# Two transformer blocks in one kernel: order of gelu and weight splits, order of the second mixer's end, and two border orders

## What is computed

```python
# first block, per layer
x = x + 0.5 * swiglu(rms(x), w_gu, w_down)         # D_FF = 2816
x = x + hybrid_mixer(rms(x))                       # gMLP branch + top-k attention, gated, @ w_out
x = x + 0.5 * swiglu(rms(x), w_gu2, w_down2)
# second block, per layer
h = mixer_2(rms(x)); x = x + rms(h)
h = conv_glu_ffn(rms(x)); x = x + rms(h)
# mixer_2
q, k, v = l2norm/silu(causal conv of 4 taps)       # gated delta rule, 4 heads of 128
o_a = rmsnorm(delta_rule(q, k, v, g, beta)) * silu(z)
o_b = softmax(q k^T / 8 + reach) v                 # 8 heads of 64, dilated attention folded into one bias
h = concat([o_a, o_b]) @ w_out
# conv_glu_ffn
gate, val = split(causal conv of 3 taps (h @ up) + bias)
h = (gelu(gate) * val) @ down
```

## Time and profile before

| | |
|---|---|
| median of three runs | 2065.92 us (2065.55 to 2076.42) |
| the profiled execution | 2066.17 us |
| its span, first to last instruction | 2064.3 us |
| mean granted TensorE clock | 0.964 of full speed |
| PE busy | 1919.4 us |
| DVE, ACT, POOL busy | 1223.1, 996.8, 652.8 us |
| second block, stage gu, layer 0 | about 1401 to 1532 us of the span |
| second block, from side's last tile to out, layer 0 | 1310.8 to 1353.8 us |
| the same in layer 1 | gu 1855 to 1985, side to out 1764.7 to 1807.7 us |

### The profile page before, as it was taken

The page is one execution under the profiler, slowest core; times in us unless marked ns, Lnnn a source line. Parts: engine busy times, 40 slices in busy tenths (PEclk is TensorE's granted clock), DMA queues, the critical chain, the costliest instruction groups (busy, mean ns, idle before and its releaser), DMA issues.

```text
span 2064.3 us, 41181 instructions
## 1 busy us (share of the span) xinstructions
PE 1919.4 (93%) x15758; PEld 1870.1 (91%) x15758; DVE 1223.1 (59%) x1478; ACT 996.8 (48%) x1304; POOL 652.8 (32%) x595
## 2 busy tenths in 40 slices
PE   6999999999999999999999989879999889779997
PEld 6999999999989999999999989769889789679897
DVE  4655586666456456866664674446664664356655
ACT  5434456544444345564444563445544564445543
POOL 4751301276137513012662016122330025032220
PEclk9999999999999999999999899989999799889999
DMA  6646444465455464444555422114445222124444
GB/s 221 209 164 210 154 144 145 162 206 193 164 195 201 157 215 164 144 146 159 206 190 168 154 102 100 42 64 144 175 144 199 90 102 87 37 82 163 166 164 159
DMA packets 49222, 314.39 MB, mean 152 GB/s; under 512 B 5713, under 2 KB 6865, under 8 KB 19921
## 3 DMA queue, kind: packets, MB, share of 16 engines
q1 hardware_dynamic: 48960, 311.09, 43.7%
q10 hardware_dynamic: 144, 1.69, 0.2%
HBM read 311.71 MB, written 1.05 MB: 152 GB/s over the span
## 4 chain that ended last, share of the span: by engine, by line
PE 62%; DVE 10%; issue 9%; ACT 9%; DMA 5%; POOL 2%; ACTq 1%; DVEq 0%; SPq 0%; POOLq 0%
PE ps L541 15%; PE ps L543 15%; PE ps L542 15%; DMA raw<-in_down_dram 4%; ACT w_hi L1109 4%; DVE w_lo L1567 4%; PE ps L858 3%; PE ps L546 3%; PE ps L547 3%; PE ps L548 3%; DVE conv L1886 2%; ACT conv L1160 2%; PE ps L691 1%; PE ps L731 1%; DVE v L2084 1%
## 5 line engine op out<-in xcount | busy, mean ns | idle before, releaser
L1567 DVE TENSOR_TENSOR w_lo<-raw,w_hi 128x2048 fp32r<-128x2048 f32 (+1 forms) x322 | 713.0, 2215 | 423.6 <-ACT w_hi L1109 423.1
L541 PE MATMUL ps<-xn,w_hi 128*128 128x256 f32 x2688 | 768.5, 286 | 59.6 <-DVE w_lo L1567 14.6
L542 PE MATMUL ps<-xn,w_hi 128*128 128x256 f32 x2688 | 755.7, 281 | 0.0
L543 PE MATMUL ps<-xn,w_lo 128*128 128x256 f32 x2688 | 755.5, 281 | 0.0
L1109 ACT ACTIVATE w_hi<-raw 128x2048 fp32r<-128x2048 f32 (+1 forms) x322 | 562.4, 1748 | 126.5 <-DMA raw<-in_down_dram 83.4
L541 PEld LDWEIGHTS ps<-xn,w_hi 128*128 128x128 f32 x2688 | 516.9, 192 | 74.2 <-issue 44.1
L542 PEld LDWEIGHTS ps<-xn,w_hi 128*128 128x128 f32 x2688 | 515.4, 192 | 0.8 <-issue 0.5
L543 PEld LDWEIGHTS ps<-xn,w_lo 128*128 128x128 f32 x2688 | 515.1, 192 | 0.0
L541 PE MATMUL ps<-h,w_hi 128*128 128x256 f32 x1056 | 294.1, 278 | 4.9 <-DVE w_lo L1567 4.8
L542 PE MATMUL ps<-h,w_hi 128*128 128x256 f32 x1056 | 293.2, 278 | 0.0
L543 PE MATMUL ps<-h,w_lo 128*128 128x256 f32 x1056 | 293.2, 278 | 0.0
(11 more groups left out here) (310 smaller groups left out, 2633.2 us busy)
## 6 DMA issues: line engine op xcount, KB each, us to landing
raw<-in_gu_dram SPq DMA_DIRECT2D x132, 1024.0 KB, 4.9
raw<-in_in_dram SPq DMA_DIRECT2D x70, 1024.0 KB, 4.9
raw<-in_down_dram SPq DMA_DIRECT2D x96, 704.0 KB, 4.1
raw<-in_out_dram SPq DMA_DIRECT2D x16, 1024.0 KB, 4.8
raw<-in_pb_dram SPq DMA_DIRECT2D x4, 1024.0 KB, 4.8
raw<-in_pa_dram SPq DMA_DIRECT2D x4, 1024.0 KB, 4.9
tables_all<-in_tables_dram ACTq DMA_DIRECT2D x1, 1648.0 KB, 7.2
rows<-in_rows_dram SPq DMA_DIRECT2D x2, 768.0 KB, 5.5
```

Of the source, the lines that this page charges most:

```text
L541: pe.matmul(out, w, xh, start=first, stop=False)
L542: pe.matmul(out, w, xl, start=False, stop=False)
L543: return pe.matmul(out, wl, xh, start=False, stop=last)
L1567: dve.tensor_tensor(w_lo[:, r, 0:elems], raw[:, k % RAW_RING, 0:elems], w_hi[:, r, 0:elems], ALU.subtract).then_inc(lo.sem, 1)
```

## The change

It has three parts. **Gelu:** `rounds` runs the body of slot j first and splits slot j+3 behind it, with one split ahead of the loop (`open_rounds`); that is the same sequence as before. What ACT has left of the body, `behind`, comes after the split: in the second block the gelu of slot j now stands behind the split of slot j+3. In the first block `open_rounds` stands ahead of ACT's root of the norm. **Mixer's end:** the units' early steps move into side's last two slots; the short units get the banks 0 to 3 and their own halves of `soft` and `p_t`; z's silu is one instruction behind `attend_exp(1)`, followed by a load of the Exp table; slots 2 and 3 of out are split ahead of the out stage; the sums over heads stand ahead of the last attention transposition, and Ln, Exp, gain and high part go by halves; PE begins out with the attention half of slots 0 to 2 in six banks, then does their delta-rule half, then slot 3 whole. The short units' helpers (`short_scores`, `short_turn`, `short_pv`, `short_mask`, `short_exp`, `short_copy`) do what the old ones did, in the other banks and buffers. **Border orders:** `tile_rounds` splits slot 2j+4 ahead of taking tile j, and takes the last two tiles behind the first split of the next stage; in the first block's out stage the split comes ahead of both tiles and the low part of tile c-1 behind the addition of tile c.

```diff
+        if k == 6:
+            attend_turn(at, 0, SC)
+        if k == 7:
+            attend_scores(at, 1, 4, SC)
...
+    def out_part(j, first, end):
+        for f in range(2):
+            if j == 3:
+                pe.wait_ge(x_new.sem, x_new.upto(at, so.free0 + f + 1))
+            for c in range(first, end):
+                if j == 0 and f == 0 and c == WC:
+                    pe.wait_ge(o_lo.sem, o_lo.upto(at, 1))
+                if j == 0 and f == 0 and c == WC + 2:
+                    pe.wait_ge(o_lo_last.sem, o_lo_last.upto(at, 1))
+                last = mac(out_tile(2 * j + f), wh[:, c, f * P:(f + 1) * P], wl[:, c, f * P:(f + 1) * P],
+                           y2[:, c, 0], y2[:, c, 1], c == 0, c == KC - 1)
+            if end == KC:
+                last.then_inc(used.sem if f else full.sem, 1)
...
+    def head_sums():
+        for b in range(2):
+            pe.matmul(ps[:, AUX + b, :], ones_q[:], q_diag[:, 2 * b:2 * b + 2].rearrange("p h q -> p (h q)"),
+                      start=True, stop=False)
+            pe.matmul(ps[:, AUX + b, :], ones[:],
+                      o_sq[:, 2 * b:2 * b + 2].rearrange("p h q -> p (h q)"), start=False, stop=True)\
+              .then_inc(o_summed.sem, 1)
...
         if k == 7:
-            attend_pv(at, 0, tok[:, V], SC)
             level_u(LEVELS - 1)
-            attend_scores(at, 1, 4, SC)
+            short_scores(at, 2)
+            short_scores(at, 3)
...
     heads4(AUX, lambda i: v_new[:, 0, i], lambda i: qk[:, 0, i], dn_out)
-    attend_out(at, 1, SC)
+    short_turn(at, 2)
     pe.wait_ge(dn_copy.sem, dn_copy.upto(at, 4))
-    attend_scores(at, 2, 4, SC)
...
     last.then_inc(dn_out.sem, 1)
-    attend_turn(at, 2, SC)
-    attend_pv(at, 2, tok[:, V], SC)
-    attend_scores(at, 3, 4, SC)
-    pe.wait_ge(q_diag_ok.sem, q_diag_ok.upto(at, 2))
-    pe.wait_ge(o_squared.sem, o_squared.upto(at, 1))
...
-    attend_turn(at, 3, SC)
-    attend_pv(at, 3, tok[:, V], SC)
-    attend_out(at, 0, SC)
-    stage_open(at, ss)
-    pe.wait_ge(o_lo.sem, o_lo.upto(at, 1))
+    attend_out(at, 1, SC)
+    short_turn(at, 3)
+    short_pv(at, 2, tok[:, V])
+    short_pv(at, 3, tok[:, V])
+    head_sums()
+    attend_out(at, 0, SC + 1)
     pe.wait_ge(yb_lo.sem, yb_lo.upto(at, 2))
-    for j in range(4):
-        wide(at, so, j, 0, y2, KC)
+    out_part(0, 0, WC)
+    out_part(1, 0, WC)
+    out_part(2, 0, WC)
+    for j in range(3):
+        out_part(j, WC, KC)
+    out_part(3, 0, KC)
@@ helpers
+    def open_rounds(at, st, split):
+split(at, st.slot0 + LEAD, 0, st.elems)
+    def rounds(eng, at, st, nxt, count, split, body, behind=None):
 def step(j, g):
-    for s in range(per):
-        split(at, st.slot0 + per * j + LEAD + s, g, st.elems)
     body(j, g)
+    split(at, st.slot0 + j + 1 + LEAD, g, st.elems)
+    if behind:
+        behind(j, g)
+cycle(eng, count - LEAD - 1, RING, step)
+for j in range(count - LEAD - 1, count):
     body(j, 0)
-    if last:
-        split(at, st.slot0 + per * j + LEAD + per - 1, 0, nxt)
+    if j == count - LEAD - 1:
+        split(at, st.slot0 + j + 1 + LEAD, 0, nxt)
+    if behind:
+        behind(j, 0)
+split(at, st.slot0 + count - 1 + LEAD, 0, nxt)
+    def tile_rounds(eng, at, st, nxt, split, body, steps=cycle):
+def step(j, g):
+    split(at, st.slot0 + 2 * j + 1 + LEAD, g, st.elems)
+    split(at, st.slot0 + 2 * j + 2 + LEAD, g, st.elems)
+    body(j, g)
+split(at, st.slot0 + LEAD, 0, st.elems)
+steps(eng, KC - 2, 2, step)
+split(at, st.slot0 + 2 * (KC - 2) + 1 + LEAD, 0, st.elems)
+split(at, st.slot0 + 2 * (KC - 2) + 2 + LEAD, 0, nxt)
+body(KC - 2, 0)
+body(KC - 1, 0)
+split(at, st.slot0 + 2 * (KC - 1) + 1 + LEAD, 0, nxt)
@@ ACT
-        else:
-            act.wait_ge(projected.sem, projected.upto(at, k + 1))
-            z = z_t[:, 2 * (k - 6):2 * (k - 6) + 2]
-            act.activation(z, z, ACT.Silu).then_inc(z_ok.sem, 1)
...
+    split(at, so.slot0 + 2, 0, SLOT)
     attend_exp(at, 1)
+    act.wait_ge(projected.sem, projected.upto(at, 8))
+    act.activation(four(z_t[:]), four(z_t[:]), ACT.Silu).then_inc(z_ok.sem, 1)
+    act.activation(warm[:, 2:3], eps[:, 0:1], ACT.Exp)
...
     out_copy(1, v_new[:, 0], AUX)
     out_copy(2, w_neg[:], AUX + 1, -1.0)
     attend_copy(at, 1, SC)
     out_copy(3, state[:], AUX)
+    split(at, so.slot0 + 3, 0, SLOT)
+    short_exp(2)
     out_copy(4, v_new[:, 1], AUX + 1)
     out_copy(5, o_t[:, :, 0:P], AUX)
-    attend_hi(at, 1, y2[:, 0:WC], SC)
-    attend_exp(at, 2)
+    short_copy(2)
+    short_exp(3)
     out_copy(6, o_t[:, :, P:T], AUX + 1)
     act.wait_ge(dn_copy.sem, dn_copy.upto(at, 6))
     act.activation(four(o_sq[:]), four(o_t[:]), ACT.Square).then_inc(o_squared.sem, 1)
-    attend_copy(at, 2, SC)
-    attend_exp(at, 3)
-    act.wait_ge(o_summed.sem, o_summed.upto(at, 1))
-    act.activation(o_rn[:].rearrange("p (b h) q -> p b (h q)", b=2), ps[:, AUX:AUX + 2, :], ACT.Ln,
-                   bias=eps[:, 1:2], scale=1.0 / P).then_inc(o_rooted.sem, 1)
-    act.wait_ge(o_rooted.sem, o_rooted.upto(at, 1))
-    act.activation(four(o_rn[:]), four(o_rn[:]), ACT.Exp, scale=-0.5).then_inc(o_inv.sem, 1)
-    attend_copy(at, 3, SC)
-    act.wait_ge(o_gated.sem, o_gated.upto(at, 1))
-    copy(y2[:, WC:KC, 0], o_t[:]).then_inc(o_hi.sem, 1)
-    attend_hi(at, 0, y2[:, 0:WC], SC)
+    short_copy(3)
+    attend_hi(at, 1, y2[:, 0:WC], SC)
+    attend_hi(at, 0, y2[:, 0:WC], SC + 1)
+    for b in range(2):
+        act.wait_ge(o_summed.sem, o_summed.upto(at, b + 1))
+        act.activation(four(o_rn[:, pair_of(b)]), ps[:, AUX + b, :], ACT.Ln,
+                       bias=eps[:, 1:2], scale=1.0 / P).then_inc(o_rooted.sem, 1)
+    for b in range(2):
+        act.wait_ge(o_rooted.sem, o_rooted.upto(at, b + 1))
+        act.activation(four(o_rn[:, pair_of(b)]), four(o_rn[:, pair_of(b)]), ACT.Exp, scale=-0.5)\
+           .then_inc(o_inv.sem, 1)
+    for b in range(2):
+        act.wait_ge(o_gated.sem, o_gated.upto(at, b + 1))
+        copy(y2[:, WC + 2 * b:WC + 2 * b + 2, 0], o_t[:, pair_of(b)]).then_inc(o_hi.sem, 1)
     for j in range(4):
-        if j < 3:
-            split(at, so.slot0 + j + LEAD, 0, SLOT)
+        if j == 1:
...
-    def gate_gelu(j, g):
+    def gate_taps(j, g):
         act.wait_ge(hv_ok.sem, hv_ok.upto(at, i - 1))
...
+    def gelu(j, g):
         act.wait_ge(conv_ok.sem, conv_ok.upto(at, 36 + 3 * j + 3 + 12 * g))
         act.activation(silu_gate[:, j % 2], conv[:, j % 2, 0], ACT.Gelu_apprx_tanh).then_inc(gate_ok.sem, 1)
-    rounds(act, at, st2["gu"], SLOT_DOWN, FC, 1, split, gate_gelu)
+    open_rounds(at, st2["gu"], split)
+    rounds(act, at, st2["gu"], SLOT_DOWN, FC, split, gate_taps, gelu)
@@ DVE
     for j in range(4):
+        if j < 3:
+            split(at, so.slot0 + j + LEAD, 0, SLOT)
         for f in range(2):
-            if f == 1 and j < 3:
-                split(at, so.slot0 + j + LEAD, 0, SLOT)
             c = 2 * j + f
             tile_done(dve, at, so, j, f)
             dve.tensor_tensor(x[:, c], x[:, c], ps[:, 2 * (j % 2) + f, 0:T], ALU.add)\
                .then_inc(x_new.sem, 1)
-            scale_low(at, 1, c, gains1[:, 3 * layer + 2, c:c + 1], xn_lo_odd if f else xn_lo_even)
+            if c:
+                low_out(c - 1)
+    low_out(KC - 1)
...
+        if k == 7:
+            attend_mask(at, 1, reach_of(T))
+        if k == 6:
+            attend_norm(at, 0, SC)
         if k == 7:
-            attend_norm(at, 0, SC)
             level_u(LEVELS - 1)
-    attend_mask(at, 1, reach_of(T))
+    split(at, so.slot0 + 2, 0, SLOT)
+    short_mask(2)
+    short_mask(3)
     attend_norm(at, 1, SC)
+    split(at, so.slot0 + 3, 0, SLOT)
     attend_lo(at, 1, y2[:, 0:WC], SC)
-    attend_mask(at, 2, reach_of(P))
-    attend_norm(at, 2, SC)
-    attend_mask(at, 3, reach_of(P))
-    dve.wait_ge(o_inv.sem, o_inv.upto(at, 1))
-    dve.scalar_tensor_tensor(four(o_t[:]), four(o_t[:]), dn_gain[:, layer], four(o_rn[:]), ALU.mult,
-                             ALU.mult).then_inc(o_norm.sem, 1)
+    attend_norm(at, 2, 1)
+    attend_norm(at, 3, 2)
+    dve.wait_ge(z_ok.sem, z_ok.upto(at, 1))
+    dve.wait_ge(dn_copy.sem, dn_copy.upto(at, 6))
+    dve.tensor_tensor(four(z_t[:]), four(z_t[:]), four(o_t[:]), ALU.mult).then_inc(o_norm.sem, 1)
+    attend_lo(at, 0, y2[:, 0:WC], SC + 1)
     dve.wait_ge(o_norm.sem, o_norm.upto(at, 1))
-    dve.wait_ge(z_ok.sem, z_ok.upto(at, 2))
-    dve.tensor_tensor(four(o_t[:]), four(o_t[:]), four(z_t[:]), ALU.mult).then_inc(o_gated.sem, 1)
-    attend_norm(at, 3, SC)
-    attend_lo(at, 0, y2[:, 0:WC], SC)
+    for b in range(2):
+        part = slice(2 * b, 2 * b + 2)
+        dve.wait_ge(o_inv.sem, o_inv.upto(at, b + 1))
+        dve.scalar_tensor_tensor(four(o_t[:, part]), four(z_t[:, part]), dn_gain[:, layer],
+                                 four(o_rn[:, part]), ALU.mult, ALU.mult).then_inc(o_gated.sem, 1)
+    dve.wait_ge(o_hi.sem, o_hi.upto(at, 2))
```

(11 more changed lines are left out.)

138 lines of the change are left out of this document (88 added, 50 removed).

## The result

The median of four runs is 1994.16 us (1990.14 to 2005.07) against 2065.74 us before: ratio 0.965, 95% interval 0.961 to 0.969. That is 71.6 us less; the forecast was 61 us, and 1994 us its low end. The profiled execution took 1990.14 us, 76.0 less than the one of before. A second group of four runs of the same changed kernel had a median of 2000.5 us: some of the difference to the forecast is scatter, and part of what follows is about what scatters.

A forecast was written before the change was run, and what follows sets the result against it. PE, busy 93% of the span, was taken as the bound, so only stages where it is not fed could gain. 2066.2 - 26.3 - 30.4 - 4 = 2005.5, stated as 2005 us; range 1994 to 2025 us.

The forecast's parts named there:

- part 1: Second block's up projection: gelu behind the split opens the ACT-DVE ring, PE becomes the bound at 5.44 us a slot; 26.3 us.
- the clock in out: Second block's out stage: a sign of success was PE's clock at 0.95 or above, where it was 0.90.
- A: Second block's up projection keeps its ring because something else ties the slots; no gain there, 2031 us; chance 0.06.
- D: Mixer's end: table loads hold ACT twice as long as shown, 5.1 us more, 2010 us; chance 0.05.
- E: Whole kernel: the new order does not bite, stages bound by something the profile doesn't show; 2066 us, chance 0.02.
- C: Second block's up projection: POOL, held off by DVE, becomes the bound and slows the kernel, up to 2119 us; chance 0.02.
- B: Mixer's end bound by ACT's queue or delta-rule steps, so PE's waits only move; 2020 to 2036 us, chance 0.15.
- part 2: Second block's mixer end, side to out and out: less PE idle time and slow clock, 15.2 us a layer, 30.4 us.
- part 3: Stage borders: first block's out 2 us, second block's down stages 2 us, ACT's split ahead of the root 0; 4 us.
- what part 2 took the clock to give back: Mixer's end, per layer: 3.7 of 4.5 us before out, one short slow stretch left, and 1.2 of up to 2.9 in out.
- The first block's out: Border behind that stage: DVE's last low parts come sooner, PE's last wait being 1.05 us; 1 us a layer, 2 in all.
- The cost of ACT's split ahead of the root: First block's norm: the split delays the root but gives the same back in DVE's low part; 0, bounds -1 and +1 us.

The follow-up runs named there:

- alone, timed: The kernel before with only the gelu move, only the mixer's end, or only the border orders: 2047.18, 2033.37 and 2060.18 us.
- The filled waits: The kernel before with 105 unread matmuls a second-block layer on PE ahead of its waits between side and out: 2057.60 us against 2067.86.
- two kinds of group: The changed kernel with four transpositions, or eight 64-column products, put on PE at every fourth slot of the second block's up projection: 2003.64 and 2020.39 us.
- the four transpositions: The changed kernel with four unread identity transpositions on PE ahead of every fourth slot of the second block's up projection: 2003.64 us, ratio 0.9677.

## Where the prediction was right, and which steps of it failed

The direction, both mechanisms, all markers of part 1 and the clock in out (1.00) came as written. Out began 23.6 us behind side's last tile, not 27 to 31: I had left the 2.8 us of moved work in that number, and the rest is the failed step below. None of the rivals A, D, E took place; C's mechanism is there without its cost. In B's place ACT's queue costs 0.4 us (`v_new`), where I had worked out 0.6. The two table loads ahead of it stand in ACT's row as 1.28 us each (1310.07 and 1312.43), and the next instruction begins 1.29 and 1.30 us behind their starts. The drain of about 1.38 us that the Trainium skill adds to a load (ScalarE: Activation LUTs, What ACT_TABLE_LOAD costs) is again not there.

| term | forecast | by the traces | alone, timed |
|---|---|---|---|
| part 1 | 26.3 | 26.7 at the fast pace, 17.8 at the slow one | 21.7 |
| part 2 | 30.4 | 37.5; 35.8 in its own run, with out at the slow pace | 35.5 |
| part 3 | 4 | not separable: the rest is 11.8 in one trace of the changed kernel and 2 in the other | 8.7 (3.5 to 13.4) |
| sum | 60.7 | 76.0 in the profiled pair | 65.9; the whole 71.6 and 67.4 |

**The step that failed first is what part 2 took the clock to give back.** I had seen the slow stretches and priced them at 4.5 and up to 2.9 us, but let "one short one be left" and took 3.7 and 1.2. None was left. The stretches of before, from side's end into out (windows as in the earlier trace rows):

```profile
1321.29:1324.70 3.41, 3.41 (x19) 3.41 (x17) 0.00 (x0) 1.57 (x4) 0.00 (x0) 0.50 0.00 0
1338.36:1341.77 3.41, 3.41 (x11) 1.79 (x11) 1.44 (x3) 0.95 (x5) 0.00 (x0) 0.50 0.00 0
1348.60:1353.80 5.20, 2.39 (x11) 1.80 (x10) 2.83 (x5) 2.85 (x3) 2.35 (x1) 0.50 0.00 0
1353.82:1358.84 5.02, 5.02 (x23) 5.02 (x24) 0.00 (x0) 0.59 (x1) 0.00 (x0) 0.50 0.00 0
```

On the way PE worked 9.2 us at half clock, which is 4.6 us more than at full clock, and in out 5.0 us, which is 2.5. By layer: from side to out 42.82 became 23.57, less the 1.73 and 1.06 us of work that moved ahead, is 16.4 us, where idle time and clock were 10.3 + 3.7 = 14.0. Idle fell from 14.0 to 2.8, not to 3.7 (0.9 us). The other 5.2 us are 4.6 of clock, not 3.7 (0.9), and 0.6 that I can't place. Out, first to last matmul, fell from 24.10 to 21.77 us, 2.3, not 1.2 (1.1); the 2.9 was too high, since that window was longer than out. That is 18.8 against 15.2 us. No wait above 1.41 us is left, and behind none of them did the clock fall. So of the some 7 us missed in two layers 4.0 are clock, 1.8 idle time and 1.2 open. The filled waits show that in out the clock is a cost of its own; on the way they gave back only 1.6 us by themselves, so that there idle time and clock are two terms of one account and not two causes shown apart.

**Two sizes in part 3 failed too, and nearly cancel.** The first block's out was sized by one wait, the 1.05 us of the earlier trace rows, where three stood in that border (1.29, 0.62 and 1.05 us, of which 0.26 is left): 2.3 to 2.7 us a layer in place of 1. The cost of ACT's split ahead of the root, 0 with bounds of 1 us, was 2.4 to 2.8 us once, at the start: I had looked at stages whose root has slack, and at the start the squares, the root and the table load are the critical path. Together they are some 2.4 us where the forecast had 2. The run alone says 8.7 us, but its interval begins at 3.5, so that more than the forecast 4 is likely and not shown. Which other borders gave more scatters too much to say: the down stages of before and after differ by less than their own spread.

**Part 1** was right to 0.4 us in the profiled pair, and that is luck, for I did not know the reason: 5.44 us a slot is PE's rate at one of two paces. The profiled execution had the fast one in both layers; with the slow one the gain is 8.9 us a layer in place of 13.4, and the seven slow and five fast stages average to 21.5 us for two layers. So the whole is a little nearer to the forecast than the profiled pair makes it.

Open: what in PE makes the two paces. That it is set by what precedes was tried with two kinds of group; that a wait sets it anew was only seen; that it is a phase, as the expectation of the four transpositions has it, was only thought. The number of operations matters too, not only their kind: in the ten traces without inserted groups the pace was the fast one behind every group of four transpositions, but the slow one behind 120 of 140 groups of eight.

## What to carry to other kernels

Where PE idles for a few microseconds, count the slow clock behind it as a separate term, and in full wherever PE is the only bound of what follows: a product that can begin with the half of its operand that is ready pays twice. When an ordering ring is taken away, ask at which rates the next bound can run and look at more than one stage and execution of it; a ring hides their scatter. At a border add up all waits of the stretch, not the last, and look at the kernel's start by itself, where a harmless reordering can stand on the critical path.
